# Two-block layer kernel: the recurrence of the delta-net heads in two chains by parity, the inverse in one PSUM bank, and the squares at the MLP's opening added on GpSimd

## What is computed

```
def hybrid_layer(x, ...):
    h = rmsnorm(x, pre_mix_g)
    dn_q, dn_k, dn_v, dn_z, dn_b, dn_a, sw_q, sw_k, sw_v, gate_a, gate_b = split(h @ w_in)
    y_a = deltanet_branch(dn_q, dn_k, dn_v, dn_z, dn_b, dn_a, ...) @ w_up_dn   # 8 heads of 128
    y_b = swa_sink_branch(sw_q, sw_k, sw_v, positions, sw_sinks) @ w_up_sw     # window of 128
    mix = (sigmoid(gate_a) * y_a + sigmoid(gate_b) * y_b) @ w_o
    x = x + rmsnorm(mix, post_mix_g)
    h2 = rmsnorm(x, pre_mlp_g)
    ff = square(relu(h2 @ w_ff1)) @ w_ff2                                       # 1024 -> 4096 -> 1024
    return x + rmsnorm(ff, post_mlp_g)
```

## Time and profile before

| what | value |
|---|---|
| median of 3 runs | 2567.79 us (2567.4 to 2571.97) |
| the profiled execution | 2566.15 us |
| its span | 2564.4 us |
| mean granted TensorE clock | 0.979 of full |
| TensorE busy | 2486.1 us, 97% of the span |
| VectorE, ScalarE, GpSimd busy | 51%, 41%, 43% |
| HBM traffic | 80 GB/s over the span |

### The profile page before, as it was taken

How to read it: one execution, slowest core, us unless ns; L and a number is a source line. 1 busy time by engine, 2 the same in 40 slices (tenths; PEclk the granted TensorE clock), 3 DMA queues, 4 the chain that set the end, 5 groups by cost and what they waited for, 6 DMA issues and landing times. The chain is left out here.

```text
span 2564.4 us, 32868 instructions
## 1 busy us (share of the span) xinstructions
PE 2486.1 (97%) x12932; PEld 2037.2 (79%) x12932; DVE 1296.6 (51%) x2164; ACT 1040.0 (41%) x2201; POOL 1106.3 (43%) x815
## 2 busy tenths in 40 slices
PE   7999999999999999989999999999999999899998
PEld 5788888777778888777888887777777788777886
DVE  4677774673431111257677646734386511466453
ACT  5555542444343223244556435433443332323332
POOL 2323233334646556433233233346465564234554
PEclk9999999999999999989999999999999999789999
DMA  3211112222222222222111121223124322352222
GB/s 129 66 50 50 50 42 66 66 66 83 90 72 93 94 96 91 73 76 65 43 58 50 42 66 60 73 83 106 60 96 131 129 97 91 116 159 92 93 92 81
DMA packets 76505, 207.56 MB, mean 81 GB/s; under 512 B 16704, under 2 KB 27712, under 8 KB 75840
## 3 DMA queue, kind: packets, MB, share of 16 engines
q1 hardware_dynamic: 76352, 205.47, 24.8%
HBM read 194.95 MB, written 10.49 MB: 80 GB/s over the span
## 5 line engine op out<-in xcount | busy, mean ns | idle before, releaser
L807 POOL TENSOR_TENSOR wL<-raw,wH 128x512 fp32r<-128x512 f32 x672 | 920.6, 1392 | 1217.0 <-ACT wH L800 1216.7
L800 ACT ACTIVATE wH<-raw 128x512 fp32r<-128x512 f32 x672 | 386.8, 623 | 788.2 <-PE ps L827 781.4
L825 PE MATMUL ps<-hH,wH 128*128 128x512 f32 (+1 forms) x1664 | 695.6, 418 | 10.2 <-DVE tmp L1591 3.8
L826 PE MATMUL ps<-hL,wH 128*128 128x512 f32 (+1 forms) x1664 | 663.1, 398 | 0.0
L827 PE MATMUL ps<-hH,wL 128*128 128x512 f32 (+1 forms) x1664 | 662.8, 398 | 0.0
L825 PEld LDWEIGHTS ps<-hH,wH 128*128 128x128 f32 (+1 forms) x1664 | 315.1, 189 | 84.5 <-issue 22.8
L827 PEld LDWEIGHTS ps<-hH,wL 128*128 128x128 f32 (+1 forms) x1664 | 314.0, 189 | 78.9 <-issue 2.0
L826 PEld LDWEIGHTS ps<-hL,wH 128*128 128x128 f32 (+1 forms) x1664 | 315.6, 190 | 61.8 <-issue 1.4
L825 PE MATMUL ps<-OH,wH 128*128 128x512 f32 x576 | 230.8, 401 | 4.6 <-DVE acc L1619 1.8
L827 PE MATMUL ps<-OH,wL 128*128 128x512 f32 x576 | 227.8, 396 | 0.0
L826 PE MATMUL ps<-OL,wH 128*128 128x512 f32 x576 | 227.8, 395 | 0.0
(11 more groups left out here) (380 smaller groups left out, 3491.3 us busy)
## 6 DMA issues: line engine op xcount, KB each, us to landing
raw<-w SPq DMA_DIRECT2D x345, 512.0 KB, 3.3
mats<-matsD SPq DMA_DIRECT2D x4, 1408.0 KB, 6.6
x<-xT SPq DMA_DIRECT2D x8, 256.0 KB, 7.9
matsD<-Cd SPq DMA_DIRECT2D x8, 256.0 KB, 2.5
matsD<-wide SPq DMA_DIRECT2D x4, 512.0 KB, 3.5
mats<-lagsD SPq DMA_DIRECT2D x32, 64.0 KB, 6.2
outT<-acc SPq DMA_DIRECT2D x8, 256.0 KB, 2.2
matsD<-tab SPq DMA_DIRECT2D x8, 128.0 KB, 1.8
```

What stands on the lines that cost most here:

```text
L800: act.activation(weights_at(slot)[0][:, k, :], raw[:, j % RAW, k, :], ACT.Copy).then_inc(high_done, 1)
L807: pool.tensor_tensor(low[:, k, :], raw[:, j % RAW, k, :], high[:, k, :].bitcast(F32), ALU.subtract).then_inc(low_done, 1)
L825: pe.matmul(out, wh, rH[:, t, :], start=(t == 0), stop=False)
L826: pe.matmul(out, wh, rL[:, t, :], start=False, stop=False)
```

## The change

**Recurrence.** B becomes two chains, even heads and odd heads, each with its own semaphore, its own S, rr, vn, osq and srow buffers and its own banks: even heads keep 4 and 5, odd heads take 7 (small products) and 3 (output). Within a chain the small products share the one place of 128x128 in their bank, and the final transposes go to the output's bank.

**D in one bank.** D has only bank 2. `turnkv` and `copykv` become turnk, copyk, turnv, copyv. `gram` and `masked` become gramk and maskk (LTm), and gramq and maskq (AT); the latter two come after `first` and `minus`. TensorE's turnv waits for ScalarE's copyk, and gramq for VectorE's minus. The doubled keys of the window branch (dupk, copyk) are done in two halves one after the other in bank 2.

**A in one bank.** p and q both go to bank 6. A of head h now waits for `minus` of D, not for D's end; B's first step waits for D's end as well.

**The opening.** GpSimd adds the squares of k-tiles 0 to 6 up in `sq_total` (a view of `rstdp`), six adds in a row, and ScalarE's square t waits for the add t-2 (the first for add 1). TensorE does no `x_sum` between the pieces; after the last piece of the first f1 tile it sums `sq_total` and the square of k-tile 7 (eight matmuls with one column in place of 32). The planner places the adds after GpSimd's split of the fourth f1 tile.

The matmuls of the heads, their shapes and their count stay the same, and so do DMAs and weight splits.

```diff
-D_STAGES = ["square", "sums", "qscale", "turnkv", "ksum", "root", "recip", "dscale", "copykv", "rows", "diff", "exps", "qdec",
-            "gram", "masked", "first", "minus"]
+D_STAGES = ["square", "sums", "qscale", "turnk", "ksum", "root", "copyk", "turnv", "recip", "dscale", "copyv", "rows", "diff", "exps",
+            "qdec", "gramk", "maskk", "first", "minus", "gramq", "maskq"]
...
-B = Count([(h, B_STAGES) for h in range(HEADS)])
+B = [Count([(h, B_STAGES) for h in range(e, HEADS, 2)]) for e in range(2)]
...
         if kind == "A" and s == "flipi":
-            out.append(last("D", j))
+            out.append(("D", j, "minus"))
         if kind == "B" and s == "v0":
-            out.append(last("A", j))
+            out += [last("A", j), last("D", j)]
...
+    chains[1:1] = [[("B", h, s) for h in range(e, HEADS, 2) for s in B_STAGES] for e in range(2)]
...
+        psS = [ps[:, 4, 0:P], ps[:, 7, 0:P]]
+        psO = [ps[:, 5, :], ps[:, 3, :]]
...
+                if t >= 2 and added == 0:
+                    act.wait_ge(sq_added, max(1, t - 2))
+                elif t >= 2:
+                    act.wait_ge(ssq_done, (1 if n else 0) + t - 1)
                 act.activation(sq[:, t % 2, :], x[:, t, :], ACT.Square).then_inc(sq_done, 1)
+
+        def square_adds(pool):
+
+            for t in range(1, KT - 1):
+                pool.wait_ge(sq_done, t + 1)
+                if t > 1:
+                    pool.wait_ge(sq_added, t - 1)
+                pool.tensor_tensor(sq_total, sq[:, 0, :] if t == 1 else sq_total, sq[:, t % 2, :], ALU.add).then_inc(sq_added, 1)
...
+        def square_sums(pe):
+
+            pe.wait_ge(sq_added, KT - 2)
+            column_sums(pe, sq_total, 0, 2)
+            pe.wait_ge(sq_done, KT)
+            column_sums(pe, sq[:, (KT - 1) % 2, :], 1, 2).then_inc(ssq_done, 1)
...
-                                ins = v.tensor_tensor(xt, xt, second_half(psA[:, 1, :], b), ALU.subtract)
+                                ins = v.tensor_tensor(xt, xt, second_half(psA[:, 0, :], b), ALU.subtract)
...
-                            if tile == OPENING[-1] and s < PARTS - 2 or tile == OPENING[0] and s >= PARTS - 2:
-                                x_sum(pe, 0, s)
+                            if tile == OPENING[0] and s == PARTS - 1:
+                                square_sums(pe)
...
-                                pe.matmul(psD[:, 0, :], k_("dup0"), kr, start=True, stop=True)
-                                ins = pe.matmul(psD[:, 1, :], k_("dup1"), kr, start=True, stop=True)
+                                ins = pe.matmul(psD[:, 0, :], k_(s[0:3] + s[-1]), kr, start=True, stop=True)
```

More of the change, by code:

```diff
@@ L312 @@
         ("pe", "G", "turn cumsum"), ("act", "G", "tanh abs expn ln expa exps"),
-        ("pe", "D", "sums rows gram turnkv"), ("act", "D", "square ksum root exps copykv"), ("pool", "D", "qdec"),
+        ("pe", "D", "sums rows gramk gramq turnk turnv"), ("act", "D", "square ksum root exps copyk copyv"), ("pool", "D", "qdec"),
         ("pe", "A", "p q turn"), ("act", "A", "copy"),
@@ L456, in needs @@
                 if j == ("ga", 0):
-                    out.append(last("B", HEADS - 1))
-            if s == "dupk":
+                    out += [last("B", HEADS - 2), last("B", HEADS - 1)]
+            if s == "dupk0":
                 out.append(last("D", HEADS - 1))
@@ L1262, in _ @@
                                 act.activation(eg, gcl[:, 0:32], ACT.Exp).then_inc(gate_stage, 1)
-                        elif kind == "D" and s in ("square", "ksum", "root", "exps", "copykv"):
+                        elif kind == "D" and s in ("square", "ksum", "root", "exps", "copyk", "copyv"):
                             act.wait_ge(gram_stage, D.before(j, s))
@@ L1330, in _ @@
                                 act.activation((OH, SH)[c % 2][:, t, :], mlp[o][:, :], ACT.Copy).then_inc(mlp_stage[o], 1)
-                        elif kind == "E" and s in ("tap3", "tanh", "copyk", "copyv", "high", "square"):
+                        elif kind == "E" and s in ("tap3", "tanh", "copyk0", "copyk1", "copyv", "high", "square"):
                             act.wait_ge(tile_stage, E.before(j, s))
@@ L1411, in _ @@
                             ins.then_inc(gate_stage, 1)
-                        elif kind == "D" and s in ("qscale", "recip", "dscale", "diff", "masked", "first", "minus"):
+                        elif kind == "D" and s in ("qscale", "recip", "dscale", "diff", "maskk", "maskq", "first", "minus"):
                             h = j
@@ L1448, in _ @@
                             if s == "flipi":
-                                v.wait_ge(gram_stage, D.end(j))
+                                v.wait_ge(gram_stage, D.before(j, "minus") + 1)
                             v.wait_ge(inverse_stage, A.before(j, s))
@@ L1510, in _ @@
                                     v.wait_ge(tile_stage, E.end(("swq", SWQ - 1)))
-                                    v.wait_ge(scan_stage, B.end(HEADS - 1))
+                                    for e in range(2):
+                                        v.wait_ge(scan_stage[e], B[e].end(HEADS - 2 + e))
                                 ins = v.stream_shuffle(qr[:, :], qraw[:, t, :], SWAP)
@@ L1572, in _ @@
                             b = ps[:, L_BANK[n], :]
-                            if s in ("tanh", "tap3", "dupk", "copyk", "turnv", "copyv", "high", "low", "square"):
+                            if s in ("tanh", "tap3", "dupk0", "copyk0", "dupk1", "copyk1", "turnv", "copyv", "high", "low", "square"):
                                 continue
@@ L1702, in _ @@
                             ins.then_inc(gate_stage, 1)
-                        elif kind == "D" and s in ("sums", "rows", "gram", "turnkv"):
+                        elif kind == "D" and s in ("sums", "rows", "gramk", "gramq", "turnk", "turnv"):
                             h = j
```

169 lines of the change are left out of this document (88 added, 81 removed), and 6 rows, old and new, of the table special.

## The result

| | before | after |
|---|---|---|
| median | 2567.6 us (2566.54 to 2571.97) | 2546.11 us (2544.19 to 2549.01) |
| profiled execution | 2566.15 us | 2544.19 us |
| its span | 2564.4 us | 2542.4 us |

The ratio is 0.9913, with a 95% interval from 0.9900 to 0.9927. Within the profiled executions it is 22.0 us, against a forecast of 9.2 (2556.95).

The account below looks back on a forecast made before the run. TensorE, 97% busy, was taken to bound the kernel. From the profiled 2566.15 us, 8.2 for the openings and 1.0 for the heads gave 2556.95; with the median 1.64 above the profiled execution, 2558.6 us, range 2550 to 2567.

Parts of the forecast that it names:

- The openings' removed work: MLP openings: six of eight x_sums go at 0.88 us each, 5.3 us per layer, 10.6 in all.
- What is late next: Openings: VectorE and GpSimd take turns, the last low part comes 1.2 us late, leaving 4.1 us gain per opening.
- my middle of 2.94: Openings: VectorE's cycle per k-tile in us, between 2.55 (each add hidden under L833) and 3.33 (none hidden).
- Two chains: Recurrence in the heads: the inverse sets the pace, so two chains cost and gain nothing.
- D and A in one bank each: Heads: new TensorE visits in D against an earlier inverse, a net gain of 0.5 us per layer.
- The bound of 5.3: Heads: TensorE's idle time per layer, 5.3 and 5.4 us, is all that a new order can take back.
- idle time taken back: Rival, heads: the new order takes back all 5.3 us per layer, the whole 2549.0 us; chance 0.12.
- the 4 to 6 of the forecast: Sign that the forecast is right: TensorE idle 4 to 6 us per layer in the heads.
- under the 2 of this rival: Sign for the rival of idle time taken back: heads with TensorE idle under 2 us.
- The clock: Rival, openings: the clock rises one group later, 1.85 to 2.3 us per opening, 2563.2 at most; chance 0.07.
- GpSimd's adds: Rival, openings: adds pace the cycle at 3.33 us, openings give 1.4 each, heads nothing, 2565.0 us; chance 0.13.
- The new visits: Rival, D in the heads: 32 visits (turnv, gramq) wait; outweighs the openings at 0.42 us each, 2575.6 at 0.5; chance 0.08.

Follow-up runs that it names:

- one_chain: The kernel after with the planner holding the recurrence in one chain over all eight heads: 2546.77 us, ratio 0.9925 to the kernel before.
- the list at 0.20: Order planned with 0.2 us as the planner's figure for a hand-over between engines, as in both main kernels: before 2567.6 us, after 2546.11 us.
- at 0.21 in place of 0.20: Both kernels with the planner's hand-over figure at 0.21 us, same instructions in another order: before 2568.43 us, after 2564.25 us.
- after_hop25: The kernel after with the planner's figure for a hand-over between engines at 0.25 us in place of 0.2: 2566.10 us.

## Why the prediction was wrong

**The openings' removed work: right.** 5.3 us per layer were to go; 5.0 and 5.6 went.

**What is late next: the mechanism right, the lateness wrong.** This is the first step that failed, by 2.4 us over the two openings. The turns of VectorE and GpSimd came, at 2.86 us per cycle with an add in it, near my middle of 2.94. What failed is "The last low part ends at 720.27 + 7 x 2.94 = 740.9: 1.2 us late", and mostly its factor of seven. VectorE adds into x one k-tile ahead of the low parts, so only six cycles lie between the first low part and the seventh, and the eighth follows alone. In the trace the low parts end at 717.69, 720.76, 723.44, 726.54, 728.90, 732.00, 734.37 and 735.26: six cycles of 2.78 on average and a last step of 0.88 us. Six cycles of 2.94 and a step of 0.74 (an estimate from the prediction's own terms) would have ended at 738.7, 1.0 us ahead of the 739.7 at which TensorE wants that low part, and the forecast for the openings would have been the 10.6 us that were measured. The rest is the price: the mean of the six is 2.78 and not 2.94, since of the six adds only three lengthened VectorE by a whole microsecond (1.77, 1.79, 1.80 for 0.74); beside the others it was 1.32, 1.01 and 1.02 for 0.69. In the kernel after the last low part ends at 735.26 and TensorE wants it at 737.4 (722.66 + 5 x 2.80 + 0.70 by the prediction's own formula): 2.1 us early and not 1.2 late.

**Two chains: right.** The second chain gives nothing, shown by one_chain, whose list is the same. The banks and buffers by parity stayed in one_chain and were not taken out alone. The inverse runs from head to head and sets the pace.

**D and A in one bank each: not a term that could be sized.** I took -0.5 per layer between -5.3 and +16; it was -3.1 and -3.9. The step that failed is "I take a net gain of 0.5 us per layer, near nothing, because D's old waits are the nearest kind"; with 6.1 us it is the largest part of the miss. As far as the runs show, the sign and size of this term don't come from waits of D, but from the whole list that the planner draws anew, and that moves the heads by several microseconds with no edit at all. Which feature of the list at 0.20 makes it good stays open. The bound of 5.3 for what could be taken back was also cut too narrowly: it is the idle time from 80 to 410, and the whole stage has 6.9. The rival "idle time taken back" (0.12) came nearest in the heads, with 2.3 and 2.5 us of idle time; its time of 2549.0 for the whole is near the result (2.9 us above it) by luck, since it takes 10.6 us from the heads, which gave 7.1, and nothing from the second block. By the prediction's own signs the heads lie between: TensorE is idle for 3.1 us of 80 to 410, neither the 4 to 6 of the forecast nor under the 2 of this rival.

**The clock.** I held it against the opening, where it changed little (the first group 4.91 us, 4.65 before). It acted 350 us and more behind the second opening, in a block that I had set to zero. The sentence "the forecast fails as a whole if other stretches move" names it, but I gave it neither a rival nor a place in the range. That is the third step that failed, a term put at nothing: 4.4 us in the trace, 2.1 in the second trace of the same program. By the table of stages the miss of 12.8 us in the profiled executions is 2.4 (openings), 6.1 (heads), 4.4 (second block), less 0.1 of rounding and start. That all three fell on the same side is in part luck: at 0.21 in place of 0.20 the same change gives 4.2 us by the medians, less than half of the forecast.

**The rivals on the slow side.** GpSimd's adds did not pace the opening. The new visits in D did not cost 0.42 us each: neither turnv nor gramq is among the waits in the heads of the kernel after, in either layer.

## What to carry to other kernels

- Where a planner rewrites the order on every edit, price the redraw before the edit: run the old kernel with another setting of the planner that changes no instruction. Here that moves the whole by 1 to 20 us, so a gain of a few microseconds in reordered code is the list's until the pair holds at several settings. The openings' gain, 10 us or more in two layers, holds at all of them (by stages; the whole moves with the rest).
- Removing steady work from a saturated engine is worth its distance between starts, and the next engine's lateness is to be worked out for the last piece that needs it, with its cycles counted in the engine's own order: here one cycle too many made all of the forecast lateness.
- A stage that runs at two clock levels changes its time when something far ahead of it changes. Its past spread belongs in the range.

## What the hardware showed beyond that

- Two added matmuls (0.47 us) ahead of a stage with frequent clock changes made it 5.8 us longer in one execution each, with the same instructions in it, and two executions of one program differ by 2.4 us there; 20 traces of the same code gave 349.6 to 358.7 us.
- A GpSimd add (1.28 us) and a VectorE add with both operands in SBUF (0.69 us) that start together cost both engines: 1.83 us for GpSimd's, and 1.77 in place of 0.74 for VectorE's next instruction.
- Short waits of TensorE in an otherwise full stretch can be followed by a fall to 1.2 GHz: 6.8 us of it behind waits of 0.81, 1.35 and 0.79 us, 3.4 us behind a single one of 0.85 and behind one of 1.70 us (after_hop25, layer 0). The same two waits in layer 1 of that trace, and one of 1.71 us in the kernel before, had no fall behind them.
